# Two attention blocks interleaved with their projections, a bias table built one stage earlier, and a reordered residual tail

## What is computed

```
q, k, v, z = split(h @ w_in)
s = q k^T / 8 ; s = where(in window, s + rel_bias[bucket(distance)], -1e30)
p = softmax([s, sink])[..., :-1] ; y = ((p v) * silu(z)) @ w_out
```

```
c_q, c_kv, k_rope, z = split(h @ w_in)          # 768, 256, 32, 1024
q = rmsnorm(c_q) @ w_uq ; k, v = rmsnorm(c_kv) @ w_ukv   (+ rotary parts)
y = (softmax(q k^T / sqrt(96)) v * silu(z)) @ w_out
```

## Time and profile before

| | us |
|---|---|
| median of 3 runs | 4081.64 |
| lowest, highest | 4078.75, 4083.47 |
| the profiled execution, its own time | 4079.84 |
| its span, first to last instruction | 4078.0 |
| TensorE busy | 3664.9 |
| VectorE busy | 2265.0 |
| GpSimd busy | 1442.0 |
| ScalarE busy | 1059.6 |

### The profile page before, as it was taken

How to read it: one execution, slowest core, us unless ns; L and a number is a source line. 1 busy time by engine, 2 the same in 40 slices (tenths; PEclk the granted TensorE clock), 3 DMA queues, 4 the chain that set the end, 5 groups by cost and what they waited for, 6 DMA issues and landing times.

```text
span 4078.0 us, 45076 instructions
## 1 busy us (share of the span) xinstructions
PE 3664.9 (90%) x15713; PEld 2819.6 (69%) x15713; DVE 2265.0 (56%) x3211; ACT 1059.6 (26%) x1707; POOL 1442.0 (35%) x700
## 2 busy tenths in 40 slices
PE   6999979899997999989899996787879989888787
PEld 5888756678875888766678885576656567556565
DVE  5443567754335443467774433785723575665736
ACT  1222223322222222223322222211223322322230
POOL 3444533444442444444444442210321034121231
PEclk9999989999998999989999998875997589898898
DMA  3333321233332333321233332312242023121220
GB/s 97 98 89 98 90 54 37 78 90 97 88 102 62 98 90 91 97 63 45 65 88 93 90 99 71 100 52 58 81 84 66 1 58 71 27 56 37 63 83 32
DMA packets 622009, 299.38 MB, mean 73 GB/s; under 512 B 96821, under 2 KB 616469, under 8 KB 621872
## 3 DMA queue, kind: packets, MB, share of 16 engines
q1 hardware_dynamic: 618256, 287.44, 25.4%
q0 software_dynamic: 2720, 7.93, 1.1%
q10 hardware_dynamic: 896, 2.23, 0.1%
HBM read 287.58 MB, written 9.96 MB: 73 GB/s over the span
## 4 chain that ended last, share of the span: by engine, by line
PE 70%; DVE 17%; issue 7%; POOL 4%; ACT 1%; DMA 0%; SPq 0%; DVEq 0%; POOLq 0%; ACTq 0%
PE ps L327 20%; PE ps L316 20%; PE ps L317 19%; PE ps L791 3%; POOL WL L257 3%; PE ps L813 2%; DVE SQ L415 2%; POOL YP L1409 1%; DVE SS L418 1%; PE ps L802 1%; PE ps L2004 1%; PE ps L2002 1%; DVE T L742 1%; DVE T L2207 1%; DVE X L747 1%
## 5 line engine op out<-in xcount | busy, mean ns | idle before, releaser
L257 POOL TENSOR_TENSOR WL<-RAW,WH 128x1024 fp32r<-128x1024 f32 (+4 forms) x606 | 1332.7, 2201 | 2486.3 <-ACT WH L279 2486.1
L316 PE MATMUL ps<-UH,WH 128*128 128x512 f32 x3120 | 1261.9, 404 | 179.7 <-DVE UL L733 54.6
L317 PE MATMUL ps<-UL,WH 128*128 128x512 f32 x3120 | 1240.2, 398 | 0.0
L279 ACT ACTIVATE WH<-RAW 128x1024 fp32r<-128x1024 f32 (+4 forms) x605 | 572.1, 946 | 1434.8 <-PE ps L327 1364.8
L316 PEld LDWEIGHTS ps<-UH,WH 128*128 128x128 f32 x3120 | 601.0, 193 | 352.6 <-issue 91.3
L327 PE MATMUL ps<-UH,WL 128*128 128x512 f32 x3120 | 801.8, 399 | 10.9 <-POOL WL L257 10.9
L327 PEld LDWEIGHTS ps<-UH,WL 128*128 128x128 f32 x3120 | 591.3, 191 | 152.3 <-POOL WL L257 14.6
L317 PEld LDWEIGHTS ps<-UL,WH 128*128 128x128 f32 x3120 | 600.6, 192 | 129.2 <-issue 3.6
L1283 DVE TENSOR_TENSOR T<-ps,R 128x512 f32<-128x512 f32 x88 | 60.9, 692 | 400.4 <-PE ps L327 400.4
L316 PE MATMUL ps<-HH,WH 128*128 128x512 f32 x704 | 279.2, 397 | 0.0
L317 PE MATMUL ps<-HL,WH 128*128 128x512 f32 x704 | 276.9, 393 | 0.0
(11 more groups left out here) (416 smaller groups left out, 3856.3 us busy)
## 6 DMA issues: line engine op xcount, KB each, us to landing
RAW<-w_ff_in SPq DMA_DIRECT2D x176, 512.0 KB, 3.8
RAW<-w_in SPq DMA_DIRECT2D x72, 512.0 KB, 3.9
RAW<-w_ff_out SPq DMA_DIRECT2D x64, 384.0 KB, 3.3
RAW<-w_ff_out SPq DMA_DIRECT2D x64, 320.0 KB, 3.1
RAW<-d_w_in SPq DMA_DIRECT2D x24, 512.0 KB, 3.8
RAW<-b_w_in SPq DMA_DIRECT2D x17, 512.0 KB, 3.9
RAW<-w_out SPq DMA_DIRECT2D x16, 512.0 KB, 4.0
RAW<-w_ple_gate SPq DMA_DIRECT2D x16, 512.0 KB, 4.0
```

The costliest lines, as they stand in the source:

```text
L257: e.tensor_tensor(m.WL[:, s, 0:k, :], m.RAW[:, r, 0:k, :], m.WH[:, s, 0:k, :].bitcast(F32), ALU.subtract).then_inc(m.low_ready.sem, 1)
L279: e.activation(m.WH[:, s, 0:k, :], m.RAW[:, r, 0:k, :], ACT.Copy).then_inc(m.high_ready.sem, 1)
L316: e.matmul(out, m.WH[:, s, c, 0:t.cols], H[:, k0 + c, :], start=(x == 0 and c == 0), stop=False)
L317: e.matmul(out, m.WH[:, s, c, 0:t.cols], L[:, k0 + c, :], start=False, stop=False)
```

## The change

- `swa`: first 7 tiles (v, both keys, query and gate tiles of chunks 0 and 1), the transposes of v in their course. Then the other 12 query and gate tiles as a `Woven`, with 58 of the 68 TensorE steps of a new thread `SinkHeads` beside them; the last 10 follow in a `Rest`. Gates are now multiplied by R first, and ScalarE's Silu of a chunk is run inside the thread, once per two heads. Head outputs go to ZH and QL, no longer to UH and UL.
- The bias table: its loads go to SyncE's list behind the load of the S5 gate product's unit 6; its matmul and scaling behind that product's tile 6; the write `skew` behind its last WL; the read `BIAS` behind the S5 output product's last WL.
- `mla`: query and key/value tiles of heads 0 and 1, then the 28 tiles of the other 14 heads as one `Woven`, with 56 of the 68 steps of a new thread `LatentHeads`; 12 follow in a `Rest`. Transposes of v share the score bank and are copied by ScalarE. The scale 1/sqrt(96) goes into RQ.
- `after_x` and `ple`: `split_gain` first, `square` second. A `Root` that isn't in chunks runs on TensorE behind its tile 0, no longer between its WH and WL matmuls. In a product with a root and one unit per tile, ScalarE makes WH one unit earlier, ahead of the tile's `act`.

```diff
@@ Gemm.scalar
+                ahead = 1 if self.root is not None and len(t.units) == 1 else 0
                 for x in range(len(t.units)):
-                    if self.iters > 1 or self.u0 + j + x + 1 < len(m.unit_k):
+                    if (n == 0 or not ahead) and (self.iters > 1 or self.u0 + j + x + 1 < len(m.unit_k)):
                         self.high(e, i, j + x + 1)
                 if self.root is not None and n == 0:
                     self.root.scalar(e)
+                if ahead and j + 2 <= self.nu and self.u0 + j + 2 < len(m.unit_k):
+                    self.high(e, i, j + 2)
@@ Gemm.tensor
-                    if root is not None and x == len(t.units) - 1 and not root.chunks:
-                        root.tensor(e)
...
                     mm.then_inc(m.unit_done.sem, 1)
+                if root is not None and not root.chunks:
+                    root.tensor(e)
                 self.tensor_tail(e, i, n)
@@ after_x
-    g.square(e, x)
     g.split_gain(e, at(m.UH, i), at(m.UL, i), x, gain)
+    g.square(e, x)
@@ the S5 gate product
+                    if j == 6:
+                        rel_load.issue(e)
...
+                def tensor_tail(self, e, i, n):
+                    if n == 6:
+                        rel.tensor(e)
...
+                def gpsimd_tail(self, e, i, j):
+                    if j == 7:
+                        e.wait_ge(m.flip_free.sem, rel.b + 1)
+                        e.dma_start(skew.rearrange("h q x -> h q x"), BROW[:].unsqueeze(1).to_broadcast([SWA_HEADS, P, 3 * P])).then_inc(skewed, 16)
...
             out_gemm(chunks(a["a_w_out_2"][0]), UF, (M2H, M2L), gg.s0)
+            add(Unskew())
@@ SinkHeads: scalar, the same order of work on the other engines as Heads
+                e.activation(B.ES[:, c:c + 1], self.sink(h), ACT.Exp, bias=B.NM[:, c:c + 1], scale=self.scale)
+                e.activation(B.S[:, c, 0:kk], B.S[:, c, 0:kk], ACT.Exp, bias=B.NM[:, c:c + 1], scale=self.scale,
+                             accum_out=B.RS[:, c:c + 1]).then_inc(m.exped.sem, 1)
...
+            if x < self.n and x % (2 * TT) == 5:
+                self.gate(e, x // (2 * TT)).then_inc(m.head_gated.sem, 1)
@@ LatentHeads
+        if n == 0:
+            m.wait_tiles(e, self.ready(h))
...
+        for t in range(lo, hi):
+            e.transpose(bank[:, (t - lo) * P:(t - lo + 1) * P], self.turn(h, t), m.IDENT[:])
...
+            e.activation(self.to(h, slice(lo, hi)), bank.rearrange("p (t x) -> p t x", x=P), ACT.Copy)
@@ swa
+            g1 = First(m, 1, [plain(VW0, KB[:, 2, :]), keys(0), keys(1), query(0), gate(0), query(1), gate(1)], rhs_ready=u_ready, root=m.chunk_root)
...
+            pace = 58
+            g2 = Woven(m, [t for c in range(2, DC) for t in (query(c), gate(c))],
+                       [(att, {"tensor": pace, "vector": pace, "scalar": pace})], rhs_ready=u_ready)
+            add(g2)
+            add(Rest(att))
+            out_gemm(chunks(a["b_w_out_2"][0]), YB, (ZH, QL), m.splits.total - DC, needs=[(m.head_out.sem, m.head_out.total)])
@@ mla
+            pair = lambda p: [query_tile(2 * p), query_tile(2 * p + 1), key_tile(2 * p), key_tile(2 * p + 1)]
...
+            add(Gemm(m, 1, pair(0)[2:] + pair(0)[:2], rhs_ready=gq.s0))
...
+            pace = 8 * (pairs - 1)
+            add(Woven(m, [t for p in range(1, pairs) for t in pair(p)],
+                      [(att, {"tensor": pace, "vector": pace, "scalar": pace})], rhs_ready=gq.s0))
+            add(Rest(att))
```

More of the change, by code:

```diff
@@ L910, in __init__, with score @@
         self.t0 = m.tiles
+    def score(self, e, h, n, x):
+        m = self.m
+        if self.b + x > 1:
+            e.wait_ge(m.exped.sem, self.b + x - 1)
+        kk = self.blocks(n) * P
+        out = m.ps[:, 2 + x % 2, 0:kk]
+        e.matmul(out, self.q(h, n), self.k(h, n), start=True, stop=False)
+        if self.add is not None:
+            w, row = self.add(h, n)
+            e.matmul(out, w, row, start=False, stop=False)
+        return e.matmul(m.ps[:, 2 + x % 2, kk - P:kk], m.IDENTB[:], self.mask, start=False, stop=True)
     def tensor(self, e):
@@ L918, in tensor @@
             if x < self.n:
[L919 to L928, removed]
+                self.score(e, *divmod(x, TT), x).then_inc(m.scored.sem, 1)
             if lag <= x < self.n + lag:
@@ L978, in vector, with values @@
         e.wait_ge(*v.last)
+    def values(self, e, h, n, x):
+        pass
     def scalar(self, e):
@@ L2209, in glu, with rel_pe, rel_vec, gpsimd @@
                 return f
+            rel_load = Load([(RELB[0:32, :], a["rel_bias_2"], swa_in), (RELB[32:33, :], a["c_masked"], swa_in), (HOT[:], a["c_hot"], swa_in),
+                             (SINK[:], a["b_sinks_2"][0].partition_broadcast(P), swa_in)])
+            def rel_pe(e, bank):
+                e.wait_ge(swa_in, 64)
+                return e.matmul(bank[0:SWA_HEADS, 0:3 * P], RELB[:], HOT[:], start=True, stop=True)
+            def rel_vec(g, e, bank):
+                e.wait_ge(*v.last)
+                e.tensor_scalar(BROW[:], bank[0:SWA_HEADS, 0:3 * P], 8.0, None, ALU.mult).then_inc(*g.frees())
+                e.wait_ge(*v.last)
+                e.wait_ge(swa_in, 64)
+                e.tensor_scalar(SINK[:], SINK[:], 8.0, None, ALU.mult).then_inc(*v.next())
+            rel = Flips(m, [(rel_pe, rel_vec)])
+            rel.t0 = 0
+            class Unskew(Step):
+                def gpsimd(self, e):
+                    e.wait_ge(skewed, 16)
+                    src = bass.AP(skew.tensor, P - 1, [[3 * P - 1, P], [P * 3 * P, SWA_HEADS], [1, 2 * P]])
+                    e.dma_start(BIAS[:], src).then_inc(skewed, 16)
             wg = chunks(a["a_w_glu_2"][0])
@@ L2271, in swa @@
-            tiles.insert(0, Tile([(lambda i: w[:, :, VW0:VW0 + P], DC, 0)], U, vec=scaled(lambda i: KB[:, 2, :])))
-            add(Gemm(m, 1, tiles, rhs_ready=u_ready))
-            for first in (0, 4):
-                add(by_four(w, ZW0 + first * P, 4, act=lambda c, first=first: (lambda e, i, pre, fun: e.activation(ZB[:, first + c, :], pre, ACT.Silu)),
-                            rhs_ready=u_ready))
-                if first == 0:
-                    add(Unskew())
-            def pe2(e, bank):
+            plain = lambda first, dst: Tile([(lambda i: w[:, :, first:first + P], DC, 0)], U, vec=scaled(lambda i: dst))
@@ L2280, in pe2, with turn_values @@
+            query = lambda c: plain(c * P, QB[:, c, :])
+            gate = lambda c: plain(ZW0 + c * P, ZB[:, c, :])
+            keys = lambda k: Tile([(lambda i: [w[:, :, KV0 + k * HD:KV0 + (k + 1) * HD]] * 2, DC, 0)], U, vec=scaled(lambda i: KB[:, k, :]), loads=2)
+            def turn_values(e, bank):
                 for t in range(TT):
@@ L2352, in vector @@
                     both = slice(NOPE, NOPE + 2 * ROPE)
+                    e.tensor_scalar(RQ[:], RQ[:], QK ** -0.5, None, ALU.mult).then_inc(*v.next())
+                    e.wait_ge(*v.last)
                     e.tensor_tensor(RT[both, :], RT[both, :], RQ[both, :], ALU.mult).then_inc(*v.next())
```

218 lines of the change are left out of this document (148 added, 70 removed).

## The result

The changed kernel takes 3986.9 us (median of 4 runs, 3983.6 to 3987.7) against 4080.5; the ratio is 0.977, with a 95% interval of 0.976 to 0.978. The gain is 94 us where 149 were forecast, and the time lies 2 us outside the range.

The account below looks back on a forecast made before the run. TensorE was taken as the bound, holding 70% of the chain of waits. Gains of 64 (local attention), 14 (bias table), 54 (latent attention) and 17 (split first) sum to 149 us: 4079.8 to 3931 us, range 3885 to 3985.

Parts of the forecast that it names:

- Local attention: Local stage: interleaving attention with 12 tiles takes 169.5 us instead of 233.6, a gain of 64 (45 to 78).
- I add 8% for waits: Local interleaved part: 139 us of TensorE work at full clock becomes 150.5 us with waits.
- 100 of 150, inside the 8%: Local interleaved part: ScalarE, with 20 us for Silu table loads, is busy 100 of 150 us, covered by the waits allowance.
- Two steps of TensorE (2.6 us) and part of a tile stand before it must wait: Local interleaved part: this TensorE work covers exponentials that come 3.2 us late behind a Silu.
- The tail: Local attention's last 10 steps, standing alone behind the tiles: 19 us (15 to 25).
- The first rival: Latent interleaving: VectorE comes late because GpSimd's WL blocks it, 28 us more, 3959 us in all; chance 16%.
- The bias table: Table write moved to the S5 output product: 18 us saved at the old place, 4 paid; gain 14 (0 to 20).
- the second rival: S5 output product: the moved write stalls it if unit 3's load lands with it, 11 us more, 3942; chance 12%.
- A wait of 1 to 6 us is left: 3: S5 output product: TensorE's remaining wait for weight loads beside the moved write, taken as 3 us.
- Split first: Product boundaries: gain product before square, root's matmul behind the first tile, shorter UL waits; gain 17 us (6 to 24).
- 7 places at 2.3: Boundaries where TensorE waits for the last UL: seven places gaining 2.3 us each, 16 in all.
- Latent attention: Latent stage: interleaving attention with 28 tiles takes 233 us instead of 286.8, a gain of 54 (30 to 75).

Follow-up runs that it names:

- the repeat: The changed kernel timed again with nothing altered: 3984.1 us, ratio 0.977 against the kernel before.
- the kernel with the tanh gate: The changed kernel with local attention's Silu written as z/2 times 1 + tanh(z/2), tanh on ScalarE and the rest on VectorE: 3971.0 us, ratio 0.974.

## Why the prediction was wrong

- **Local attention** is the term that failed, and the only one outside its own range: 64 forecast (45 to 78), 20 measured (233.6 less 213.7). Interleaving did lift the clock, from 0.51 to 0.91, and without it the stage is 24 to 25 us longer. The step that failed is "I add 8% for waits", with its "100 of 150, inside the 8%". It weighed ScalarE's busy time and not the order in which its work stands. The 33 us missing in the interleaved part are, on TensorE's timeline: waits of 21.8 us instead of 11.5; twelve tiles in 81.6 us instead of 65.3, of which 13.9 are matmuls that follow each other at more than the 0.227 us that they keep at full clock, a cost that the forecast did not have, and 2.4 the 24 changes from tile to attention; attention's own steps in 80.6 where 74 were forecast. "Two steps of TensorE (2.6 us) and part of a tile stand before it must wait" fell with it: each of the seven Silus in the part has a wait some 3 us behind, 0.72 us at three of them and 2.69 to 2.77 at four. Two causes are shown by taking them away: the table loads gave 11 us back and the halved WL 6. With both gone the waits are at 11.9, the 8% of the forecast, yet the part still takes 166.6 instead of 150.5: 76.0 for the tiles (8.5 of it slower matmuls, 2.3 the changes) and 78.7 for attention, with 17 us at half clock. What keeps the clock down there, and attention 5 us longer, stays open.
- **The tail** was sized from whole steps of 1.3 to 2.55 us; it took 29.8, 11 more than forecast, at a clock of 0.71. Leaving fewer steps for it made it 18.7, at a price of some 6 us in front of it.
- **VectorE and GpSimd.** The first rival had the mechanism, but in the wrong stage. In the latent part halving WL gave nothing, as the text against that rival (banks and slack) would have it. In the local part, where a step takes TensorE 1.4 us (80.6 / 58) and one blocked operation lasts 2.5, it cost 7 us, by the halves. The scaling's interleaved 965 against 486 was the sign.
- **The bias table.** 21.6 us saved in the local stage (18 forecast) and 10.7 paid in front of it (4 forecast): a gain of 11 for 14, which is nearer than either part was. The forecast had the right unit: unit 3's load had landed at 2891.7, unit 4's stood beside the write. So the second rival's condition did not come true; its price, 11 us, did. The step that failed is "A wait of 1 to 6 us is left: 3". The wait was 6.34, the unit behind it took 2.35 us more at a mean clock of 0.69, for which the sum has no term though rows 8 were read that way at the old place, and the product's first tiles came 1.9 later (1 forecast). The issue also went out late: GpSimd waited 7.01 us for VectorE's row, and its next WL stood behind. By an estimate, the write would have landed at about 2921 (2928.0 less 7.0) without this, and the load and its WH would have been ready some 2.7 us behind, before TensorE reached the unit at 2924.5; no run shows that.
- **Split first.** Waits for UL fell from 16.6 to 5.4, as forecast ("under 8"). The gain up to S5's input is 9.0 for 16. At five boundaries (behind a first swiglu, a mixer or a gate) the tiles start 1.5 to 3.9 us earlier, 13 in all. At the two behind a second swiglu there was next to no UL wait to win (0.70 and 0.69 us before), and the tiles start 1.8 and 0.95 later; 1.8 more went in the first layer's mixer, where profiles of the same code differ by as much (0.0 to 4.2). The step "7 places at 2.3" counted places that were not alike, and "(1.4, two operations of 0.69, is the least)" was wrong for two of them. In the latent input the moved root costs 2.4.
- **Latent attention.** 54 forecast, 57.6 measured; point by point this working held, with TensorE waiting for VectorE's evacuations next to nothing (one wait of 1.3 us).
- **S5.** 5.2 us were lost where nothing is edited. The same instructions took 266.5 to 274.5 us in ten profiles of kernels with this S5 stage, 274.5 and 271.9 in the changed kernel's two (the repeat was made to see this), at clocks from 0.75 in the fastest to 0.71 in the slowest. The one profile of the kernel before, 269.3, lies within them. So the 5.2 are no sign of an effect of the change.

The sum of what is named: 44 us of the 55 that are missing lie in local attention, 7 in the table's write, 7 in split first, 5 in S5; what else came out otherwise than forecast gives 7 back on balance. All low ends together would have given 3999 us, and the measured time lies under that; the range was cut to 3985 because "the ends don't fall together", and one term alone missed by 44.

## What to carry to other kernels

When two engines' work is interleaved by a written order, price not the busy share but the longest single instruction that can stand in the loop of dependencies (a table change, a blocked operation), against the length of one step; and price what comes behind the wait, since waits of 2.7 to 3.2 us were followed here by matmuls at half clock. Where GpSimd streams through SBUF beside a busy VectorE, make its instructions short: that alone gave 0.4% in both kernels. Two edits at a boundary may each give nothing alone and gain together, so test them in pairs.

## What the runs showed of the hardware

- Where VectorE is stopped beside GpSimd's WL, the stop lasts for what is left of GpSimd's instruction, however small the operation: even the sum of one column, 0.15 us elsewhere, took 1.86. With every WL halved, 208 stretched operations began beside a first half and ended beside the second, so VectorE does get in between. Three did not: they took 5.4 to 5.9 us beside four halves in a row, where in the changed kernel they took 5.1 to 5.6 beside two whole ones; why is open. Not every operation is stopped. In the changed kernel the scalings, casts, sums and products that were stretched all have their tensors in SBUF. Row maxima out of PSUM (128x512) took at most 0.69 us in 14 cases beside a WL, the reciprocal of one column at most 0.17 in 44, both as without it. In the timelines of the kernel with the tanh gate:

```profile
3045.52 2.53 POOL L257 TENSOR_TENSOR WL<-RAW,WH 128x1024 fp32r<-128x1024 f32 x1 [11.36 <-ACT WH L279]
...
3046.21 1.86 DVE L1043 TENSOR_TENSOR RSUM<-RSUM,ESINK 128x1 f32<-128x1 f32 x1
```

- A weight load issued 3.6 us behind the 3 MB write (2897.5 against 2893.9) landed at 2929.6, 32 us after its issue and 1.6 us after the write had landed (2928.0), where the profile's page has 3.8 to 4.1 us for loads of its size. With an eighth of the write there was no such wait. What the write cost was the load queued beside it.
- A table load takes 1.28 us. It began 0.02 us behind the instruction ahead of it in all 15 cases between 3020 and 3210 us, and the next instruction began 0.01 behind the load in 14 of them (the first load stood ready 5.4 us early).
